# Five of six pairs of modulation vectors on VectorE as folded row sums, in tasks between the dense units

## The chip, the cores and the metric

The kernel runs on one core of a Trainium2 chip. The metric is the device time of one execution in microseconds (us). A core has TensorE (PE: matrix products, written to PSUM), VectorE (DVE), ScalarE (ACT), GpSimd (POOL) and SyncE (SP), which here only issues DMAs. Each engine runs its own instructions in order; they wait for each other by semaphores.

## The reference

A network of two layers and a closing block for 512 tokens of width 1024, with 256 context tokens beside them. The change touches only the modulation vectors:

```python
for l in range(DEPTH):                       # DEPTH = 2, D = 1024
    mod = silu_c @ w_ada[l] + b_ada[l]       # (1, 1024) @ (1024, 6144)
    sh1, sc1, gt1, sh2, sc2, gt2 = [m[:, None, :] for m in jnp.split(mod, 6, axis=-1)]
    modc = silu_cc @ w_ada[l] + b_ada[l]     # the same for the context
    shc1, scc1, gtc1, shc2, scc2, gtc2 = jnp.split(modc, 6)
    hc = modulate(rmsnorm(xc, g_mix[l]), shc1, scc1)
    h = modulate(rmsnorm(x, g_mix[l]), sh1, sc1)      # h * (1 + scale) + shift
    p = h @ w_in[l]
    x = x + gt1 * latent_mixer(p, ...)                # attention, convolution, gates, w_out
    h2 = modulate(rmsnorm(x, g_ffn[l]), sh2, sc2)
    x = x + gt2 * expert_choice_ffn(h2, ...)          # router, 16 experts
    # the context goes the same way in layer 0; in layer 1 it only gives keys and values
```

## The kernel before

**Stages.** For each layer: projection (one "values" unit, ten rotary units `("r", n)`, twelve convolution units `("c", fp, part, f)`), attention, merge (24 gate units `("g", br, d)`, numbered t = 8·br + d, after every second of them one branch unit `("b", br, d)` of two products; then eight output units `("o", d)`), choice (norm, router product, softmax, top-k, gathering of rows) and experts. The closing block follows. Layer 0 works on T = 768 columns (tokens and context), layer 1 after its keys on 512.

**A dense unit** is 128 output features: its weights (512 KB) come from HBM into the ring, ScalarE rounds them into a high part (`act_high`, L556), VectorE takes the difference as a low part (`dve_low`, L565), and TensorE multiplies high·high, high·low and low·high over eight slices of 128 rows (`pe_linear3`, L592: 48 matmuls of 512 or 256 columns at T = 768). The parts have two buffers: unit u+1 can be rounded once unit u−1 is multiplied, so VectorE's low part has one unit's length of room, less what ScalarE takes.

**The ring** has six slots of 512 KB (`halves`). SyncE issues the DMAs in the order of the list that `mixer_weights` builds, and piece p waits until piece p−6 has been read (`sp_dense`). A split piece is free when VectorE has taken its low part, a modulation piece when its product is done. Behind the list of layer 0 SyncE loads expert weights (`sp_experts`): three places of the old ring when they are free, four more once TensorE has done the second norm's sum, the rest after the gather.

**Modulation.** Both layers' vectors are made in layer 0. They are six pairs (pair = 3·layer + n2) of 2048 columns of `w_ada`, each 16 tiles of 128 x 1024: `pe_mod` (L665) multiplies a tile with the 32-column operand `csv` (column 0 the silu of c, column 1 that of c_ctx, the rest zero), four matmuls that run side by side on 32 columns of the array, and accumulates in one PSUM bank over eight tiles; `act_mod` (L675) copies the bank to SBUF, `pe_modt` (L683) turns it (four transposes), and `dve_mod` (L694, L700) adds the bias and makes the gain. Pair 0 is done in the start. Tiles 16 to 47 (pairs 1 and 2) follow two by two behind the ten rotary units and the first six convolution units, tiles 48 to 63 (pair 3) two by two in the first eight gate units, tiles 64 to 67 behind the last output unit, and 68 to 95 (the rest of pair 4 and pair 5) stand in `pe_choice`: 68 to 79 ahead of the router product (L1498), 80 to 87 ahead of its sum (L1507), 88 to 95 and pair 5's turn ahead of the product that turns the top-k indices (L1536 on).

**VectorE** has, by stage: in a convolution unit of part 2 the four operations L1029 to L1038, in one of part 0 the product L1043; in the gates the weighing L1429 (GpSimd adds the weighed product to the sum, L1471); in an output unit the update L1459 (GpSimd adds squares, L722). After the convolution it goes into the attention, whose first step is the row maximum L1094.

## Time and profile before

| what | value |
|---|---|
| median of 3 runs | 3527.2 us (3522.58 to 3527.33) |
| profiled execution: time / span | 3522.45 us / 3520.6 us |
| mean granted TensorE clock | 0.978 of full speed |
| busy: TensorE, weight loads, VectorE, ScalarE, GpSimd | 3278.1, 2200.8, 1242.5, 1004.9, 221.8 us |
| chain that ended last, by engine | TensorE 81%, DMA 10%, VectorE 4%, ScalarE 3%, issue 1% |
| HBM read | 606.54 MB |

The page cuts the span into 40 slices of 88 us; a digit is a share in tenths, 9 is 90% or more:

```profile
PE   6999999999799999989999996988879999989998
DVE  3335642233401011145563333111125444353333
PEclk9999999999799999999999998999999999989999
DMA  7540014221999999743102329999983121323331
```

Slices 1 to 4 hold the start and the projection of layer 0, 4 to 6 its attention, 6 to 10 its merge, 11 its choice, 11 to 18 its experts; layer 1's merge ends in slice 24, and its experts fill slices 25 to 30. The chain of waits is the part of the profile that says what the end of the span hung on: it starts at the last instruction and goes back, at each step to what released it. A view by time gives start, duration and, in brackets, how long the engine sat idle and for whom.

### The profile page before, as it was taken

The numbers are of one execution on the slowest core, as the hardware profiler recorded it, in microseconds if no ns is written. First come the engines' busy times: TensorE is split into PE (matmuls) and PEld (weight loads), VectorE is DVE, ScalarE is ACT, GpSimd is POOL, SyncE is SP. The second block draws the span as 40 slices with busy tenths as digits, with TensorE's granted clock in tenths as the row PEclk, the third lists the DMA queues.
The fourth block names the chain that finished last, engine by engine and source line by source line (L and its number), as shares of the span: only waits on it lengthen the run. The fifth ranks groups of instructions, "written<-read, shape, count | busy, mean of one in ns | idle before, by whom it ended". The sixth has DMA issues, their size and how long they took to land.

```text
span 3520.6 us, 48007 instructions
## 1 busy us (share of the span) xinstructions
PE 3278.1 (93%) x21250; PEld 2200.8 (63%) x21250; DVE 1242.5 (35%) x1821; ACT 1004.9 (29%) x1571; POOL 221.8 (6%) x142
## 2 busy tenths in 40 slices
PE   6999999999799999989999996988879999989998
PEld 5787667888334343467768882332328766858887
DVE  3335642233401011145563333111125444353333
ACT  3623541122210001037353222000022354342223
POOL 0100000121000000001000220000002010120000
PEclk9999999999799999999999998999999999989999
DMA  7540014221999999743102329999983121323331
GB/s 216 151 143 25 1 49 122 64 61 59 335 398 399 385 350 395 298 64 81 42 1 72 97 90 369 421 421 421 421 327 87 35 58 37 96 60 97 101 96 66
DMA packets 385614, 617.00 MB, mean 175 GB/s; under 512 B 99234, under 2 KB 288896, under 8 KB 360704
## 3 DMA queue, kind: packets, MB, share of 16 engines
q1 hardware_dynamic: 378064, 596.50, 47.9%
q0 software_dynamic: 4384, 15.73, 1.3%
q8 instruction: 168, 2.75, 0.3%
q10 hardware_dynamic: 2960, 1.71, 0.2%
q14 instruction: 38, 0.31, 0.0%
HBM read 606.54 MB, written 7.34 MB: 174 GB/s over the span
## 4 chain that ended last, share of the span: by engine, by line
PE 81%; DMA 10%; DVE 4%; ACT 3%; issue 1%; POOL 0%; ACTq 0%; SPq 0%; DVEq 0%
PE ps L592 32%; PE ps L1844 6%; PE ps L2228 5%; PE ps L1083 4%; DMA ring<-in_w_e_up 4%; PE ps L1172 3%; PE ps L1880 3%; PE ps L1847 3%; DMA ring<-in_w_e_down 3%; PE ps L1133 3%; PE ps L644 3%; PE ps L1347 3%; PE ps L1839 2%; PE ps L613 2%; PE ps L1885 2%; PE ps L1876 2%
## 5 line engine op out<-in xcount | busy, mean ns | idle before, releaser
L592 PE MATMUL ps<-xh,wh 128*128 128x512 f32 x1912 | 638.2, 372 | 19.4 <-DVE xl L2074 9.3
L592 PE MATMUL ps<-xl,wh 128*128 128x512 f32 x1912 | 630.7, 368 | 0.0
L592 PE MATMUL ps<-xh,wl 128*128 128x512 f32 x1912 | 630.2, 368 | 0.0
L565 DVE TENSOR_TENSOR wl<-ring,wh 128x1024 fp32r<-128x1024 f32 (+1 forms) x259 | 333.1, 1287 | 443.0 <-ACT wh L556 441.4
L592 PEld LDWEIGHTS ps<-xh,wh 128*128 128x128 f32 x1912 | 330.6, 189 | 101.3 <-issue 23.8
L556 ACT ACTIVATE wh<-ring 128x1024 fp32r<-128x1024 f32 (+1 forms) x259 | 271.9, 1050 | 421.1 <-PE ps L592 161.7
L592 PEld LDWEIGHTS ps<-xh,wl 128*128 128x128 f32 x1912 | 330.6, 189 | 61.0
L592 PEld LDWEIGHTS ps<-xl,wh 128*128 128x128 f32 x1912 | 330.2, 189 | 58.7 <-issue 0.5
L1844 PE MATMUL ps<-ring,arena 128*32 128x512 f32 x1344 | 177.6, 600 | 0.9 <-ACT arena L1592 0.9
L1839 PE MATMUL ps<-ring,arena 128*64 128x512 f32 x704 | 163.2, 605 | 12.4 <-DMA ring<-in_w_e_up 8.0
L1094 DVE TENSOR_REDUCE sm<-ps 128x2 f32<-128x1536 f32 (+3 forms) x96 | 142.3, 1482 | 42.0 <-PE ps L1083 41.6
L1083 PE MATMUL ps<-arena 64*128 64x256 f32 (+3 forms) x800 | 150.9, 451 | 2.6 <-DVE arena L1043 1.8
L1112 ACT ACTIVATE tmp<-ps,sm 128x768 f32<-128x768 f32 (+3 forms) x176 | 132.7, 763 | 46.5 <-DVE sm L1097 39.0
L1133 PE MATMUL ps<-consts,tmp 128*128 128x128 f32 x832 | 126.8, 284 | 20.5 <-DVE arena L1189 12.2
L2005 DVE SCALAR_TENSOR_TENSOR y<-ps,aff,y 128x1024 fp32r<-128x1024 f32 x16 | 20.5, 1284 | 306.9 <-ACT y L1936 306.9
L1471 POOL TENSOR_TENSOR arena<-arena,tmp 128x768 f32<-128x768 f32 (+1 forms) x32 | 65.8, 2059 | 980.5 <-DVE tmp L1429 980.5
L1133 PEld LDWEIGHTS ps<-consts,tmp 128*128 128x128 f32 x832 | 88.3, 141 | 59.0 <-issue 21.8
L1839 PEld LDWEIGHTS ps<-ring,arena 128*64 128x64 f32 x704 | 48.4, 138 | 115.5 <-issue 80.4
L1876 PE MATMUL ps<-ring,arena 128*64 128x512 f32 x360 | 93.7, 596 | 21.7 <-DMA ring<-in_w_e_down 13.7
L1172 PE MATMUL ps<-arena 128*64 128x256 f32 (+1 forms) x896 | 99.6, 368 | 14.6 <-DVE arena L1156 14.6
L1156 DVE COPY arena<-ps 128x512 f32<-128x512 f32 (+1 forms) x136 | 87.2, 657 | 69.9 <-PE ps L1133 69.9
L1083 PEld LDWEIGHTS ps<-arena 64*128 64x128 f32 (+1 forms) x800 | 86.8, 187 | 38.0 <-issue 28.4
(277 smaller groups left out, 4437.1 us busy)
## 6 DMA issues: line engine op xcount, KB each, us to landing
ring<-in_w_e_gate SPq DMA_DIRECT2D x87, 1024.0 KB, 19.7
ring<-in_w_e_up SPq DMA_DIRECT2D x85, 1024.0 KB, 20.2
ring<-in_w_e_down SPq DMA_DIRECT2D x85, 1024.0 KB, 20.7
ring<-in_w_in SPq DMA_DIRECT2D x112, 512.0 KB, 3.9
ring<-in_w_ada SPq DMA_DIRECT2D x96, 512.0 KB, 4.9
arena<-in_w_e_up SPq DMA_DIRECT2D x43, 1024.0 KB, 17.7
arena<-in_w_e_down SPq DMA_DIRECT2D x43, 1024.0 KB, 20.1
arena<-in_w_e_gate SPq DMA_DIRECT2D x41, 1024.0 KB, 20.4
```

Of the source, the lines that this page charges most:

```text
L556: e.activation(in_heads(X, u, m.WH[:, o:o + many]), heads_of(X, u, halves.aps[s], many), ACT.Copy).then_inc(*hi.up(X.key, q))
L565: e.tensor_tensor(in_heads(X, u, m.WL[:, o:o + many]), heads_of(X, u, halves.aps[s], many), in_heads(X, u, m.WH[:, o:o + many].bitcast(F32 ...
L592: i = e.matmul(ps[0:M, a:b], w[:, k, 0:M], h[:, k, a:b], start=k == 0 and p == 0, stop=k == 7 and p == 2)
L1083: x = e.matmul(ps[:, col:col + k.shape[-1]], q, k, start=first, stop=last, skip_group_check=True)
L1094: e.tensor_reduce(mx, A.units(i, A.scores(i)), AX, ALU.max).then_inc(*a_rm.up(A.stage, i))
L1112: e.activation(dst[:, u], src[:, u], ACT.Exp, bias=A.small(i, 1)[:, u:u + 1], scale=s["scale"], accum_out=A.small(i, 2)[:, u:u + 1]).then_ ...
L1133: x = e.transpose(ps[:, 128 * c:128 * c + 128], src[:, u, 128 * b:128 * b + 128], ident)
L1172: e.matmul(ps[r0:r0 + 64, q0:q1], v, pt, start=x == 0, stop=x == len(pv) - 1, skip_group_check=True)
L1839: i = e.matmul(pa[64 * h:64 * h + 64, 512 * w:512 * w + 512], rows_of(1, kk, x, 0, 64), W[:, k, 512 * h:512 * h + 512], start=kk == 0, sto ...
L1844: e.matmul(pa[64 * h + g:64 * h + g + 32, 512 * w:512 * w + 512], rows_of(0, kk, x, g, g + 32), W[:, k, 512 * h:512 * h + 512], start=kk = ...
L1876: i = e.matmul(ps[64 * x:64 * x + 64, 512 * h:512 * h + 512], HT2[p % 2][:, x, k % 4, k // 4, :], w, start=k == 0, stop=k == 7)
L2228: i = e.matmul(ps[:, n:n + 512], ff_part(h, f)[c], w[:, 0, n:n + 512], start=f == 0 and p == 0, stop=f == 31 and p == 2, skip_group_check= ...
```

## The change

Pair 0 stays as it is. The other five pairs leave TensorE: each is cut into four groups of 512 columns (20 groups, `MODS`), and a group into five tasks. Tasks 0 to 3 each take a piece of 256 rows x 512 columns (512 KB, as before; 80 pieces as before) and add the rows, scaled by `csv`, into an accumulator of 128 x 512: for each of two slices of 128 rows and each vector one VectorE operation, `scalar_tensor_tensor` (the first slice `tensor_scalar`). Pairs 1 to 3 have two vectors, pairs 4 and 5 one (layer 1's context needs none of theirs). Task 4 (the turn) does for each vector a transpose of 128 x 512 in blocks of 32 x 32 and a row sum over 32 columns (128 x 16 remains). When a pair's four groups are done, `pe_fold` adds the four blocks of partitions by four matmuls of 32 (or 16) columns with the widened constant `fold`, and `dve_fold` adds the bias and makes the gain.

The tasks stand at the end of the VectorE work of single units: layer 0's convolution units (2, 1 or 2 tasks for part 1, 2, 0; pair 1), layer 0's gate units (2 in even t, 1 in odd t, none in t = 7 and 15) and output units 0 to 2 (2 each) for pairs 2 and 3; layer 1's convolution units 0 to 9 (1 each) and gate units (30 tasks from t = 0 to 20) for pairs 4 and 5. The pieces stand in the ring's list behind the weights of the unit after; no modulation piece is left in the rotary units, behind the output units or in the choice stage. Folds: in layer 0 at t = 0, t = 16 and output unit 5, in layer 1 at t = 8 and 22. ScalarE's five copies go.

```diff
+        MR0 = TR = tmp[:, 3840:4352]
+        ACC = [tmp[:, 4352 + 512 * i:4864 + 512 * i] for i in (0, 1)]
+        RS = tmp[:, 5376:5632].rearrange("p (s q w b) -> p s q w b", s=2, q=4, w=2)
+        MODS = [(pair, q) for pair in range(1, 6) for q in range(4)]
+        vectors = lambda g: (0, 1) if MODS[g][0] < 4 else (0,)
...
+        def mod_quarter(g, c):
+            pair, q = MODS[g]
+            o = 2048 * (pair % 3) + 512 * q
+            return piece(I["w_ada"][pair // 3][256 * c:256 * c + 256, o:o + 512])
+
+        def spread(groups, slots):
+            tasks = iter([(g, c) for g in groups for c in range(5)])
+            return {slot: [x for _, x in zip(range(many), tasks)] for slot, many in slots}
+
+        beside_conv = lambda many: [(("c", j), many[j // 2 % 3]) for j in range(12)]
+        beside_gates = [(("t", t), 0 if t in (7, 15) else 2 - t % 2) for t in range(24)]
+        TASKS = [{**spread(range(4), beside_conv((2, 1, 2))),
+                  **spread(range(4, 12), beside_gates + [(("o", d), 2) for d in range(3)])},
+                 {**spread(range(12, 14), [(("c", j), int(j < 10)) for j in range(12)]), **spread(range(14, 20), beside_gates)}]
+        FOLDS = [{("t", 0): 1, ("t", 16): 2, ("o", 5): 3}, {("t", 8): 4, ("t", 22): 5}]
...
+            for m in range(16) if l == 0 else ():
+                X.raw(("mod", m), *mod_source(m), p_mod, "mod", m)
+
+            def mods(parts):
+                for g, c in parts:
+                    if c == 4:
+                        continue
+                    X.raw(("mods", g, c), *mod_quarter(g, c), d_md, "mod", g, 2 * c + 1, vectors(g)[-1])
...
-                if j < 16:
-                    mods(16 + 2 * j, 17 + 2 * j)
+                if j > 9:
+                    mods(TASKS[l]["c", j - 10])
...
-                    if t < 8:
-                        mods(48 + 2 * t)
...
+                    mods(TASKS[l]["t", t])
             for d in range(KD):
                 X.split(("o", d), 128, column(I["w_out"][l], 128 * d))
-            mods(*range(64, 96))
+                mods(TASKS[l].get(("o", d - 1), []))
...
+        def dve_mod_part(e, X, g, c):
+            if c == 4:
+                return dve_mod_turn(e, g)
+            s, srcs, many, kind, what, arrived = X.pieces[X.plain["mods", g, c]]
+            e.wait_ge(*arrived)
+            for k in (2 * c, 2 * c + 1):
+                src = halves.aps[s][:, 512 * (k % 2):512 * (k % 2) + 512]
+                for w in vectors(g):
+                    if k == 0:
+                        if g:
+                            e.wait_ge(*d_md.at("turn", g - 1, w if w in vectors(g - 1) else 0))
+                        e.tensor_scalar(ACC[w], src, csv[:, 0, w:w + 1], None, ALU.mult).then_inc(*d_md.up("mod", g, k, w))
+                        continue
+                    e.wait_ge(*d_md.at("mod", g, k - 1, w))
+                    e.scalar_tensor_tensor(out=ACC[w], in0=src, scalar=csv[:, k, w:w + 1], in1=ACC[w], op0=ALU.mult,
+                                           op1=ALU.add).then_inc(*d_md.up("mod", g, k, w))
+
+        def dve_mod_turn(e, g):
+            pair, q = MODS[g]
+            if q == 0 and pair > 2:
+                e.wait_ge(*p_modt.at("mod", pair - 2))
+            for w in vectors(g):
+                e.wait_ge(*d_md.at("mod", g, KD - 1, w))
+                if w or g:
+                    e.wait_ge(*(d_md.at("sum", g, 0) if w else d_md.at("sum", g - 1, vectors(g - 1)[-1])))
+                e.transpose(TR, ACC[w]).then_inc(*d_md.up("turn", g, w))
+                e.wait_ge(*d_md.at("turn", g, w))
+                e.tensor_reduce(RS[:, pair % 2, q, w], TR.rearrange("p (b i) -> p b i", i=32), AX, ALU.add).then_inc(*d_md.up("sum", g, w))
+
+        def pe_fold(e, pair):
             ps, when = bank.take(("modt", pair), d_mod.at("mod", pair, 1))
             for w in when:
                 e.wait_ge(*w)
-            e.wait_ge(*c_mod.at("mod", pair))
-            for c in range(4):
-                i = e.transpose(ps[:, 128 * c:128 * c + 128], MR(pair)[:, 128 * c:128 * c + 128], ident)
+            g = MODS.index((pair, 3))
+            many = len(vectors(g))
+            e.wait_ge(*d_md.at("sum", g, many - 1))
+            sums = RS[:, pair % 2, :, 0:many].rearrange("p q w (k g) -> p g q w k", g=4)
+            for g in range(4):
+                i = e.matmul(ps[32 * g:32 * g + 32, 0:16 * many].rearrange("p (q w k) -> p q w k", q=4, w=many), K("fold"), sums[:, g],
+                             start=True, stop=True)
             i.then_inc(*p_modt.up("mod", pair))
 
-        def dve_mod(e, pair):
+        def dve_fold(e, pair):
             l, n2 = pair // 3, pair % 3
+            many = len(vectors(MODS.index((pair, 3))))
             e.wait_ge(*p_modt.at("mod", pair))
-            pv = bank.of["modt", pair][:, 0:512].rearrange("p (n h g w) -> p n g h w", n=2, h=2, g=4)
-            for nb in (0, 1):
-                j0 = 16 * n2 + 8 * nb
-                o = modv[:, l, j0:j0 + 8, :].rearrange("p (g h) w -> p g h w", h=2)
-                b = PT[:, 32 + 48 * l + j0:40 + 48 * l + j0].rearrange("p (g h) -> p g h", h=2)
-                e.tensor_tensor(o, pv[:, nb, :, :, 0:2], b.unsqueeze(3).broadcast_to([128, 4, 2, 2]),
-                                ALU.add).then_inc(*d_mod.up("mod", pair, nb))
+            ps = bank.of["modt", pair][:, 0:16 * many].rearrange("p (q w k) -> p q k w", q=4, w=many)
+            o = modv[:, l, 16 * n2:16 * n2 + 16, 0:many].rearrange("p (q k) w -> p q k w", q=4)
+            b = PT[:, 32 + 48 * l + 16 * n2:48 + 48 * l + 16 * n2].rearrange("p (q k) -> p q k", q=4)
+            e.tensor_tensor(o, ps, b.unsqueeze(3).broadcast_to([128, 4, 4, many]), ALU.add).then_inc(*d_mod.up("mod", pair, 1))
             if n2 != 1:
-                m = n2 // 2
-                g = PT[:, 16 * m + 8 * l:16 * m + 8 * l + 8].unsqueeze(2).broadcast_to([128, 8, 2])
-                e.wait_ge(*d_mod.at("mod", pair, 1))
-                e.scalar_tensor_tensor(out=A1v[:, l, m], in0=modv[:, l, 24 * m + 8:24 * m + 16, :], scalar=1.0, in1=g,
-                                       op0=ALU.add, op1=ALU.mult).then_inc(*d_mod.up("mod", pair, "A"))
+                dve_gain(e, pair, many)
...
-                    if l == 0 and t == 8:
-                        pe_modt(e, 3)
                     pe_linear3(e, X, ("g", br, d), 128, T, (X.key, "g", t), g_sg.at(X.key, t))
-                    if l == 0 and t < 8:
-                        pe_mod(e, 48 + 2 * t)
+                    if ("t", t) in FOLDS[l]:
+                        pe_fold(e, FOLDS[l]["t", t])
...
+                if ("o", d) in FOLDS[l]:
+                    pe_fold(e, FOLDS[l]["o", d])
...
+                for task in TASKS[l]["c", j]:
+                    dve_mod_part(e, X, *task)
...
+                    if ("t", t - 1) in FOLDS[l]:
+                        dve_fold(e, FOLDS[l]["t", t - 1])
...
+                    for task in TASKS[l]["t", t]:
+                        dve_mod_part(e, X, *task)
...
+                for task in TASKS[l].get(("o", d), []):
+                    dve_mod_part(e, X, *task)
+                if ("o", d - 1) in FOLDS[l]:
+                    dve_fold(e, FOLDS[l]["o", d - 1])
...
-            mods(*range(68, 80))
...
-            mods(*range(80, 88))
...
-            mods(*range(88, 96))
-            if l == 0:
-                pe_modt(e, 5)
...
-                act_mod(e, 4)
```

## Rows read from the trace of the kernel before

**Rows 1.** Groups of instructions: shapes xcount | busy us, mean ns | idle, releaser.
```profile
L665 PE MATMUL ps<-ring,cs 128*32 128x256 f32 x768 | 57.7, 409 | 13.3 <-DMA ring<-in_w_ada 13.1
```

**Rows 2.** TensorE by time, one rotary unit: start us, us, what.
```profile
106.78 1.07 PE L665 MATMUL ps<-ring,cs 128*32 128x256 f32 x16
107.78 1.56 PE L889 MATMUL ps<-tmp,consts 128*128 128x512 f32 x4
```

**Rows 3.** Chain of waits, convolution units of layer 0: start us, us, what.
```profile
205.76 8.68 PE ps L592 x48
215.43 8.68 PE ps L592 x48
...
253.58 42.42 PE ps L592 x240
```

**Rows 4.** Chain of waits, gate units of layer 0.
```profile
521.25 8.67 PE ps L592 x48
...
549.40 8.68 PE ps L592 x48
...
596.47 8.66 PE ps L1347 x48
608.72 18.34 PE ps L592 x96
627.06 8.46 PE ps L1347 x48
...
652.48 8.48 PE ps L1347 x48
```

**Rows 5.** Chain of waits, router stage of layer 0, in its own window.
```profile
898.74 2.63 PE ps L1498 x32
...
902.27 6.78 DMA ring<-in_w_ada
...
909.73 1.46 PE ps L1507 x12
...
923.37 7.85 DMA ring<-in_w_ada
```

**Rows 6.** Chain of waits, whole span, its 195 longest pieces: neighbours around the experts.
```profile
936.67 8.19 DMA taken<-h2d,aff
1492.29 3.47 PE ps L1880 x16
```

**Rows 7.** Chain of waits, router stage of layer 1: its ends.
```profile
2104.78 9.09 PE ps L592 x40
...
2159.90 9.57 PE ps L1839 x32
```

**Rows 8.** VectorE by time, router stage of layer 0: the normalised rows.
```profile
887.76 8.56 DVE L1629 SCALAR_TENSOR_TENSOR arena<-arena,A,tmp 128x512 f32<-128x512 f32 x16 [6.59 <-ACT tmp L753]
```

**Rows 9.** VectorE groups by form: shapes xcount | busy us, mean ns.
```profile
L918 DVE STREAM_SHUFFLE tmp<-tmp 128x512 f32<-128x512 f32 x32 | 23.5, 734 | 0.0
...
L2079 DVE SCALAR_TENSOR_TENSOR tmp<-arena,PT,tmp 128x512 f32<-128x512 f32 x16 | 18.1, 1141 | 6.0 <-ACT tmp L753 5.6
...
L1034 DVE SCALAR_TENSOR_TENSOR tmp<-tmp,PT 128x511 f32<-128x511 f32 x8 | 6.0, 751 | 0.3
```

**Rows 10.** VectorE by time, one convolution product unit.
```profile
214.47 0.95 DVE L1029 TENSOR_TENSOR tmp<-tmp,ps 128x768 f32<-128x768 f32 x1 [6.66 <-PE ps L592]
...
218.23 1.22 DVE L565 TENSOR_TENSOR wl<-ring,wh 128x1024 fp32r<-128x1024 f32 x1
```

**Rows 11.** VectorE by time, a low part in the second gate branch.
```profile
636.71 2.87 DVE L565 TENSOR_TENSOR wl<-ring,wh 128x1024 fp32r<-128x1024 f32 x1
```

**Rows 12.** GpSimd by time, the same moment.
```profile
636.66 1.84 POOL L1471 TENSOR_TENSOR arena<-arena,tmp 128x768 f32<-128x768 f32 x1 [1.49 <-DVE tmp L1429]
```

**Rows 13.** All engines by time, entry of the first attention.
```profile
296.03 0.95 DVE L1043 TENSOR_TENSOR arena<-tmp,ps 128x768 f32<-128x768 f32 x1 [6.10 <-PE ps L592]
...
298.74 1.76 DVE L1094 TENSOR_REDUCE sm<-ps 128x2 f32<-128x1536 f32 x1 [1.76 <-PE ps L1083]
```

107 lines of the change are left out of this document (40 added, 67 removed).

## The prediction

> **What bounds the kernel now.** I read the chain of waits first, then TensorE by time where the modulation stands, then VectorE in the units that get the tasks. The chain is TensorE for 81% of the span, and in layer 0's dense units it is TensorE without a gap. So a microsecond of products taken from those units is a microsecond of time, as long as nothing else ends last there. In the choice stage the chain is another: twice it stands on the arrival of a piece of `w_ada` for about 7 us [rows 5], while TensorE's own work is short. In layer 0's experts TensorE bounds again: after the gather the next long piece of the chain that isn't one of many short TensorE pieces comes at 1492 us, and no DMA stands between [rows 6]. So what is won ahead of the experts should stay won, though the stage reads weights at nearly the rate of the queues (385 to 399 GB/s on the page).
>
> A group view is of little use for the size: it gives the modulation products 57.7 us of busy time [rows 1], but they overlap their neighbours, and a third of them lies in the choice stage.
>
> **What is removed.**
>
> *Rotary units.* Two tiles begin at 106.78 and the next product begins at 107.78: 1.00 us for two tiles [rows 2]. Ten units: 10.0. Pair 1's turn in one of them goes too, 0.4 by its four transposes (half of what two tiles take, as an estimate). Cover: the next unit's weights are rounded in time here: nothing of VectorE's or ScalarE's releases L592 in these units, so the gain is taken whole. **10.4 us.**
>
> *Convolution units.* With two tiles the units follow each other at 9.67 us; five units without tiles take 42.42, which is 8.48 each [rows 3]. The difference is 1.19, six times, and a turn of 0.4: **7.6 us.**
>
> *Gate units, first branch.* Two gate units and a branch unit with four tiles take 28.15 us (521.25 to 549.40); without tiles 25.42 (627.06 to 652.48) [rows 4]. 2.73, four times: **10.9 us.**
>
> *Between the branches.* The branch unit at 596.47 ends at 605.13, its last tile at about 605.7, and the next gate unit only begins at 608.72 [rows 4]. ScalarE's high part for that unit is queued behind its copy of pair 3's products, which waits for the last tile; both go. That is 3.0 us, and 1.4 more, since the two units that follow take 18.34 us instead of 2 x 8.48 [rows 3, 4]: TensorE had stood still and began again at the lower of its two clocks. **4.4 us.**
>
> *Choice stage.* 64 to 67 go from behind the output units: about 1.0 on the chain. The rows of the router product are ready when VectorE has passed them on (887.76 + 8.56 = 896.3) [rows 8] and ScalarE about 0.8 later (768 columns, an estimate by VectorE's rate for them); the product then needs some 0.7 at the lower clock, the copy 1.0 and the sum up to 2.0, so the sum would end near 900.7 less the 1.0 above, 899.7. It ended at 909.73 + 1.46 = 911.19 [rows 5]. That is 11.5 in all. The last tiles waited until 923.37 + 7.85 = 931.2 [rows 5], and pair 5's copy and turn behind them put off the product that turns the indices by 1.9, counted from the end of the top-k. Then the gather: 8.19 us from issue to landing [rows 6], while seven expert pieces of 1 MB, issued at the same moment, share the queues. With the list 16 MB shorter these are in before the gather starts. The gather alone: bounds 0 and 4.5 us less (nearest are single 512 KB pieces of weights at 3.9 us in the page's issues); I take 3. **16.4 us.** As a cross-check, layer 1's choice stage without tiles takes 2159.90 - 2113.87 = 46.0 [rows 7]. With its sizes for 768 instead of 512 columns I get 51 for layer 0, which now takes 67.4. That is 16 too.
>
> Sum of the gains: 10.4 + 7.6 + 10.9 + 4.4 + 16.4 = **49.7 us.**
>
> **What is added.**
>
> *The price of a task.* A multiply-add of 128 x 511 takes 0.751 us [rows 9]. Two vectors alternate, so one needn't wait for the one before it. Of 512 and 256 columns, sixteen unchained ones take 8.56 us [rows 8]; by columns that is 0.66 for 512 with the overlap. A product task with two vectors is 4 x 0.66 = 2.65; with one vector the two are chained, 2 x 0.79 = 1.6. A block transpose isn't in the trace. Bounds: half and twice the shuffle across the same 32 rows, which has 0.734 [rows 9]; as the nearest row I take that, and the same for the row sum. A turn is then 2 x 1.5 = 3.0, with one vector 1.5. In all 12 x (4 x 2.65 + 3.0) + 8 x (4 x 1.6 + 1.5) = some 226 us of VectorE.
>
> *Room in the convolution units.* In a unit of part 2 VectorE works from 214.47 to 218.23 behind the unit's end and then takes the low part, 1.2 [rows 10]. Laid out unit by unit with 8.48 for each: 3.9 + 3.0 (a turn) + 1.2 = 8.1 of 8.48; part 0: 1.1 + 5.3 + 1.2 = 7.6, with a turn 8.0; part 1 is free sooner. So each task just fits, and nothing or 1 us is lost; I take **0.5**. With turns of 4.5 the same layout loses 3.5.
>
> *Entry of the attention.* The last convolution unit has two tasks (2.65 + 3.0), and they stand on VectorE ahead of the first row maximum, which began at 298.74, 1.8 after the unit's product ended [rows 13]. It would begin at 297.0 + 5.65 = 302.7: 4.0 later, and everything in the attention waits for it. With 0.5 for TensorE's clock after the longer pause: **4.5.** This is the dearest of the added parts.
>
> *Gates of layer 0.* The tightest place is the branch unit's low part: from the end of the last unit VectorE has its weighing 1.1, one task 2.65, a low part 1.2, two tasks 5.3 and a low part 1.2 = 11.5 of the 17.0 that two gate units take. GpSimd adds the weighed product in the second and third branch, and the row shows what that does: a low part took 2.87 us instead of 1.22 [rows 10, 11] where an addition of 1.84 ran from the same moment [rows 12]. That is 1.65 more: 13.1 of 17.0. Nothing is lost. The Trainium skill, "SBUF — State Buffer", section "Who interferes with whom", says why: a VectorE instruction with two SBUF inputs contends with a GpSimd instruction that reads SBUF, and one blocks while the other runs. The rule speaks against this change, since every multiply-add here has two SBUF inputs; by it as by the rows the loss per unit is at most one addition of GpSimd.
>
> *Output units.* Here it decides: 1.3 for the update, 5.3 to 5.65 for two tasks, 1.2 for the low part and up to 1.7 for GpSimd's sum of squares is 9.5 to 9.9 of 8.35 in units 1 and 2. By the order of the units the second overrun only adds what the first didn't already give: **2.2**, with the last gate unit's task ahead of the last low parts.
>
> *Layer 1.* Gates: room as above. Convolution: a unit has 5.5 us (two thirds of 8.3); own work 2.7 by columns, a turn 1.5 and the low part 1.2 fill it, with a few tenths over: **0.5.**
>
> *Folds.* Four small matmuls each, about 0.5, five times: **2.5.** The DMA amount is unchanged (80 pieces of 512 KB); layer 1 gets 16 MB where the page shows under 100 GB/s, and its expert prefetch hangs on TensorE's norm sum, not on the list.
>
> Sum of the costs 0.5 + 4.5 + 2.2 + 0.5 + 2.5 = **10.2.** Net 39.5, so 3522.45 - 39.5 = **3483 us** for an execution like the profiled one, which lies 5 below the median of the runs and at their lowest.
>
> **Rivals.**
>
> *A, deeper: 3473.* The gather lands in half the time, the folds vanish in the stream, and the units keep the faster pace that the rotary units show (8.32 against 8.48, cause unknown). For: nothing competes for the queues any more. Against: the pace isn't tied to anything that the change touches.
>
> *B, VectorE late in places: 3494.* A transpose at its upper bound or dearer multiply-adds lengthen turns to 4.5: 3.5 in the convolution, 1.5 at the attention, 3 in the output units, 3 in layer 1. For: the room is 0.4 us in the convolution. Against: shuffle and multiply-add rows.
>
> *C, the choice stage's gain is given back in the experts: 3499.* They begin 16 us earlier, and the queues, not TensorE, then set their pace. For: the rate on the page. Against: seven pieces are in sooner, and no DMA is on the chain today [rows 6].
>
> *D, slower: 3542.* VectorE ends last in every unit that has tasks. A multiply-add of the same size takes 1.141 us in another access pattern [rows 9]. At that price a task is 4.6, and a gate cycle runs into its branch unit: 1.1 + 4.6 + 1.65 + 1.2 + 9.1 + 1.2 = 18.9 of 17.0, 1.9 lost twelve times, 23; by the same layout 10 in the convolution, 9 in the output units and attention, 17 in layer 1. These 59 come on top of the forecast, 3483 + 59, so 20 slower than before. Units run over from about 1.0 per multiply-add on, and the gain is gone near 1.1. Against: these tiles are contiguous, as those of the 0.751 row.
>
> *E, no change: 3522.* What went from TensorE was hidden anyway. Against: the paces with and without tiles [rows 3, 4].
>
> The Trainium skill, "VectorE: DVE Perf Modes", section "Rules for kernel authors", advises to restructure a `tensor_reduce` on a hot path as the slowest operation; no row of a 512-column row sum from SBUF is in this trace, and B is what would follow.
>
> **How the numbers follow.** Forecast 0.62, A 0.13, B 0.14, C 0.05, D 0.04, E 0.02. The likeliest time is 3483; its own range is 3476 to 3490. The range for 8 in 10 reaches over A and into B: 3469 to 3497. A measurement of this kernel can tell about 0.2% from no change. Faster by more than that: 0.94; within it 0.02; slower 0.04.
>
> **What would show it.** Right: no wait of TensorE on `w_ada`; convolution and rotary units at the pace without tiles; the first row maximum some 6.7 us after the last convolution unit; router stage near 51 us; VectorE busy near 1465 us. A wrong step shows as idle time of TensorE ahead of L592 released by VectorE's low part (B, D) or by a DMA in the experts (C), and as the duration of the multiply-add, the transpose and the row sum. I would be wrong above all if these run slower than their nearest rows, or if the tasks' pieces, freed by VectorE, hold up weights behind them in the ring.

## The result, and the profile after the change

| what | before | after |
|---|---|---|
| median | 3526.93 us (3522.58 to 3527.33) | 3484.86 us (3480.73 to 3485.78) |
| ratio | | 0.9879, interval 0.9867 to 0.9892 |
| span of the profiled execution | 3520.6 us | 3483.8 us |
| VectorE busy | 1242.5 us | 1442.8 us |
| TensorE busy | 3278.1 us | 3233.3 us |
| mean granted TensorE clock | 0.978 | 0.980 |

The kernel became 1.2% faster: 3483 was forecast, 3484.86 measured. The spans of the two profiled executions differ by 36.8 us where the steps of the prediction give 39.5.

First the page of the kernel after: busy time of the engines, the chain by engine, and the groups of the new VectorE work (shapes and count | busy us, mean ns of one | idle time before).

```profile
PE 3233.3 (93%) x20626; PEld 2182.4 (63%) x20630; DVE 1442.8 (41%) x2136; ACT 1002.0 (29%) x1566; POOL 226.2 (6%) x142
...
PE 80%; DMA 9%; DVE 6%; ACT 3%; issue 1%; POOL 0%; ACTq 0%; SPq 0%; DVEq 0%
```

```profile
L735 DVE SCALAR_TENSOR_TENSOR tmp<-ring,cs,tmp 128x512 f32<-128x512 f32 x224 | 167.4, 796 | 1.9
...
L746 DVE STREAM_TRANSPOSE tmp<-tmp 128x512 f32<-128x512 f32 x32 | 22.6, 707 | 0.5
L748 DVE TENSOR_REDUCE tmp<-tmp 128x16 f32<-128x512 f32 x32 | 21.9, 686 | 1.1
```

VectorE got 228 us of new instructions (these rows and 15.9 of the first slices' L732; 226 was the sum of the prediction) and is busy 41% of the span, and still ends last in only 6% of the chain. Its busy time is 1442.8 us where the prediction looked for 1465; 14.5 of the missing 22 are the low parts, which took 333.1 us before and 318.6 after. The block transpose and the row sum, for which the trace before had no row, take 0.707 and 0.686 us; the shuffle at 0.734 in [rows 9] was a good neighbour for both.

Then the chain of waits of the kernel after (start us, us, what), at the places of [rows 3] (convolution), [rows 4] (gates), [rows 5] (choice) and [rows 6] (gather).

```profile
176.55 101.77 PE ps L612 x576
...
480.79 8.59 PE ps L612 x48
...
506.63 16.95 PE ps L612 x96
523.58 8.32 PE ps L1398 x48
...
582.43 16.95 PE ps L612 x96
...
838.96 17.18 PE ps L612 x96
...
874.75 1.50 PE ps L1551 x12
...
899.90 4.14 DMA taken<-h2d,aff
```

The twelve convolution units stand there as one piece of 101.77 us, which is 8.48 each: no task of VectorE made TensorE wait in them. The output units end at 838.96 + 17.18 = 856.14. A gate cycle (two gate units and a branch unit) takes 25.27 instead of 28.15. Between the branches nothing stands still: 582.43 follows the branch unit of 574.11 + 8.32. No arrival of `w_ada` is on the chain, and the gather lands after 4.14 us instead of 8.19.

By stage, each from the start of its first dense unit in the chain to that of the next stage (the output units are counted from the end of the last branch unit to their own end):

| stage | before | after | gain | forecast |
|---|---|---|---|---|
| start, to the first rotary unit | 77.88 | 79.74 | -1.9 | none |
| rotary units | 108.88 | 96.81 | +12.1 | +10.4 |
| convolution units | 109.24 | 101.77 | +7.5 | +7.6 - 0.5 |
| attention, to the first gate | 197.02 | 202.47 | -5.5 | -4.5 |
| gates, first branch, and boundary | 115.70 | 101.64 | +14.1 | +10.9 + 4.4 - 0.5 |
| gates, second and third branch | 203.0 | 202.6 | +0.4 | -0.5 |
| output units | 68.3 | 71.1 | -2.8 | -2.2 - 0.5 |
| choice, to the first expert product | 67.4 | 50.4 | +17.0 | +16.4 |
| experts of layer 0 and norm | 601.2 | 600.9 | +0.3 | 0 |
| layer 1, values to first gate | 318.9 | 321.2 | -2.3 | -0.5 |
| the rest of layer 1 | | | -2.1 | -1.0 |

(A fold is 0.5, as the prediction has it, five times.) The last line is the 36.8 of the spans less the 38.9 by which the first gate of layer 1 begins earlier.

### The profile page after: what moved, and what is told of

Same layout as the page of the kernel before. It is cut to its first block, busy times and chain, and to the rows that moved or that the text cites. A ratio compares the mean times of both kernels' runs of the same rounds, so it can differ in the third digit from the quotient of the medians.

```text
span 3483.8 us, 47130 instructions
## 1 busy us (share of the span) xinstructions
PE 3233.3 (93%) x20626; PEld 2182.4 (63%) x20630; DVE 1442.8 (41%) x2136; ACT 1002.0 (29%) x1566; POOL 226.2 (6%) x142
## 4 chain that ended last, share of the span: by engine, by line
PE 80%; DMA 9%; DVE 6%; ACT 3%; issue 1%; POOL 0%; ACTq 0%; SPq 0%; DVEq 0%
PE ps L612 32%; PE ps L1876 6%; PE ps L2260 5%; PE ps L1134 4%; DMA ring<-in_w_e_up 4%; PE ps L1223 3%; PE ps L1912 3%; PE ps L1879 3%; PE ps L664 3%; DMA ring<-in_w_e_down 3%; PE ps L1184 3%; PE ps L1398 3%; PE ps L1871 2%; PE ps L633 2%; PE ps L1917 2%; PE ps L1908 2%
## 5 line engine op out<-in xcount | busy, mean ns | idle before, releaser
L585 DVE TENSOR_TENSOR wl<-ring,wh 128x1024 fp32r<-128x1024 f32 (+1 forms) x259 | 318.6, 1230 | 296.6 <-ACT wh L576 295.9
L1871 PE MATMUL ps<-ring,arena 128*64 128x512 f32 x704 | 163.1, 605 | 12.7 <-DMA ring<-in_w_e_up 8.1
L735 DVE SCALAR_TENSOR_TENSOR tmp<-ring,cs,tmp 128x512 f32<-128x512 f32 x224 | 167.4, 796 | 1.9
L1223 PE MATMUL ps<-arena 128*64 128x256 f32 (+1 forms) x896 | 99.6, 368 | 14.6 <-DVE arena L1207 14.6
```

Source lines behind the costliest of these rows:

```text
L585: e.tensor_tensor(in_heads(X, u, m.WL[:, o:o + many]), heads_of(X, u, halves.aps[s], many), in_heads(X, u, m.WH[:, o:o + many].bitcast(F32 ...
L735: e.scalar_tensor_tensor(out=ACC[w], in0=src, scalar=csv[:, k, w:w + 1], in1=ACC[w], op0=ALU.mult, op1=ALU.add).then_inc(*d_md.up("mod", g ...
L1223: e.matmul(ps[r0:r0 + 64, q0:q1], v, pt, start=x == 0, stop=x == len(pv) - 1, skip_group_check=True)
L1871: i = e.matmul(pa[64 * h:64 * h + 64, 512 * w:512 * w + 512], rows_of(1, kk, x, 0, 64), W[:, k, 512 * h:512 * h + 512], start=kk == 0, sto ...
```

## The experiments

Each kernel ran beside the kernel before on the same chip. The median of the kernel before was 3524.93 us (3523.24 to 3525.91) beside the first four kernels, 3527.9 (3523.26 to 3530.19) beside the next four and 3525.71 (3519.71 to 3528.32) beside the last two. So medians of different groups can be compared to some 3 us only; a smaller difference from the changed kernel rests on the stages of the chains.

**What do the five pairs still cost?** The first kernel leaves pairs 1 to 5 out, products and loads, so layer 1 and the second half of layer 0 compute with shift and gate 0 and gain 1.

```diff
             def mods(parts):
-                for g, c in parts:
+                for g, c in ():
...
         def dve_mod_part(e, X, g, c):
+            return
...
```

> The changed kernel with pairs 1 to 5 left out altogether (no load, no task, no fold; their shifts and gates are zero and their gains one), so it shows what is won by taking the products away, without the price of what replaced them. Theory: the stretches of the changed kernel without its own losses, 5.5 at the attention, 2.8 in the output units, 1.6 in layer 1's convolution and 1.5 to 2.5 for the folds: about 3472 (51 below before; the prediction's sum of gains was 49.7). Rival (products largely hidden, and the added work costs nothing): about 3484.

Measured: 3472.39 us (3471.54 to 3473.22), ratio 0.9851 (0.9835 to 0.9867), span 3471.4. As expected (3472): without the pairs the kernel before would be 52.5 us shorter, and the form on VectorE costs 12.5 of that by the medians (3484.86 - 3472.39) and 12.4 by the spans (3483.8 - 3471.4); by the two ratios it is some 10. The chain of this kernel says where:

```profile
176.55 101.77 PE ps L612 x576
...
476.71 17.23 PE ps L612 x96
...
781.85 66.81 PE ps L612 x384
...
892.44 4.05 DMA taken<-h2d,aff
...
1592.42 65.33 PE ps L612 x288
```

The convolution is as long as in the changed kernel, so 20 tasks cost nothing there. The first gate comes 4.1 us sooner, and that is the attention alone. From there to the end of the output units it is 371.95 against 375.35: 3.4. The gather is the same. Layer 1 is 2.5 shorter up to its first gate, and its twelve convolution units are one piece of 65.33; the rest is 2.1 shorter.

**Is the attention's loss the queue on VectorE?** The second kernel moves the last four tasks of pair 1 from convolution units 10 and 11 to the first gate units; the later tasks move up, so that gate units 1, 3, 5 and 7 have one more. The group that lies half on either side of the attention is overwritten there, so that part of pair 1 isn't computed as in the reference.

```diff
-        TASKS = [{**spread(range(4), beside_conv((2, 1, 2))),
-                  **spread(range(4, 12), beside_gates + [(("o", d), 2) for d in range(3)])},
+        many_conv = [2, 2, 1, 1, 2, 2, 2, 2, 1, 1, 0, 0]
+        many_gate = [2, 2, 2, 2, 2, 2, 2, 1, 2, 1, 2, 1, 2, 1, 2, 0, 2, 1, 2, 1, 2, 1, 2, 1]
...
-        FOLDS = [{("t", 0): 1, ("t", 16): 2, ("o", 5): 3}, {("t", 8): 4, ("t", 22): 5}]
+        FOLDS = [{("t", 4): 1, ("t", 16): 2, ("o", 5): 3}, {("t", 8): 4, ("t", 22): 5}]
```

> The changed kernel, but the last four tasks of pair 1 (three products' worth and the turn) stand in gate units 0 and 1 instead of convolution units 10 and 11; the later tasks of the gates move up, with one more task in t = 1, 3, 5 and 7, and pair 1's fold stands at t = 4. Theory (the entry of the attention): VectorE's 5.4 us of tasks ahead of the first row maximum are what the attention lost, so the stretch from the end of the last convolution unit to the first gate unit falls from 202.5 back to about 197.5 us, and the time from 3484.9 to about 3480. Rival (the attention lost its 5.5 us to something else, the clock or the ring): the stretch stays within 1 us of 202.5 and the time within 1 us.

Measured: 3480.93 us (3479.76 to 3484.74), ratio 0.9878 (0.9861 to 0.9894), span 3479.7. The medians lie 3.9 apart, the spans 4.1; the ratios (0.9878 and 0.9879) don't tell the two kernels apart. The evidence is the stretch from the last convolution unit to the first gate, which went from 202.5 to 198.4, where 197.5 was expected. What it lost in the changed kernel shows in VectorE and TensorE by time (start us, us, engine, line; in brackets idle time and what ended it):

```profile
278.34 0.95 DVE L1093 TENSOR_TENSOR arena<-tmp,ps 128x768 f32<-128x768 f32 x1 [1.09 <-PE ps L612]
279.21 2.73 DVE L735 SCALAR_TENSOR_TENSOR tmp<-ring,cs,tmp 128x512 f32<-128x512 f32 x4
...
281.86 0.70 DVE L746 STREAM_TRANSPOSE tmp<-tmp 128x512 f32<-128x512 f32 x1
...
284.67 1.75 DVE L1145 TENSOR_REDUCE sm<-ps 128x2 f32<-128x1536 f32 x1
...
287.78 0.69 PE L1184 MATMUL ps<-consts,tmp 128*128 128x128 f32 x2 [5.58 <-ACT tmp L1163]
```

The product of the unit is taken over at 278.34, and then one task and a turn run, 5.5 us, ahead of the first row maximum. This begins 6.4 us after the unit's end; before it was 2.7 [rows 13]. TensorE stands still for 5.6 us and waits for ScalarE, which waits for that maximum.

That is 3.6 us, and the stretch lost 5.5. The rest goes with TensorE's granted clock, which can be read in the eleven profiles without doubled multiply-adds. These rows take the 18 us from the end of the last convolution unit on; the number behind the brackets is the granted clock. They are of the kernel before, the kernel with no pairs, the changed kernel, and two that come below: the fifth (no task ahead of the attention) and the kernel before with cut products.

```profile
296.00:314.00 18.00, 13.94 (x99) 1.00 0.00 1
278.32:296.32 18.00, 14.30 (x90) 0.91 0.01 1
278.32:296.32 18.00, 11.20 (x52) 0.81 0.28 83
279.21:297.21 18.00, 13.93 (x99) 1.00 0.00 1
297.28:315.28 18.00, 14.59 (x80) 0.81 0.01 1
```

| tasks ahead of the attention | granted clock in the 18 us | attention, to the first gate |
|---|---|---|
| none: before, fourth and fifth kernel | 1.00 | 197.0, 196.8, 196.8 |
| none: no pairs, tasks moved, last design | 0.91 | 198.4, 198.4, 198.1 |
| none: before with cut products | 0.81 | 199.5 |
| two: changed kernel (twice), third kernel, held pieces | 0.81 | 202.5, 202.3, 202.2, 202.3 |

Without tasks at the entry the clock falls to its lower level in some executions and not in others, even of the same code (first and third line), and that costs 1.0 to 2.5 us. With the two tasks it fell in all four profiles. So the changed kernel's 5.5 are 3.6 of queue and some 1.8 of clock.

**Are the output units' tasks free in fuller gates?** The third kernel takes all tasks out of the output units and the last gate unit, and puts a second task into the odd gate units of branches 0 and 1.

```diff
...
+        many_gate = [2, 2, 2, 2, 2, 2, 2, 1, 2, 2, 2, 2, 2, 2, 2, 0, 2, 1, 2, 1, 2, 1, 2, 0]
+        many_out = [0, 0, 0]
...
+        FOLDS = [{("t", 0): 1, ("t", 16): 2, ("o", 1): 3}, {("t", 8): 4, ("t", 22): 5}]
```

> The changed kernel, but without tasks in gate unit 23 and in the output units; these seven stand in odd gate units (two tasks each in t = 1, 3, 5, 9, 11 and 13, one in 7), and pair 3's fold at output unit 1. Theory (the output units overrun because tasks and GpSimd's additions stand ahead of the low parts): end of the last branch unit to end of the last output unit falls from 71.1 to about 68.3 us, the time by about 3 to 3482. The fuller gate units don't lose anything (13.1 + 2.65 of 17.0 by the prediction's layout). Rival (VectorE has no room in the gates either): what is won there is lost in the gate units, and the time stays or rises.

Measured: 3484.91 us (3482.02 to 3485.57), ratio 0.9886 (0.9869 to 0.9902), span 3482.4, no shorter than the changed kernel by the medians. The expectation was wrong in two places. The output units fell from 71.1 to 70.1, where 68.3 was expected, and from the first gate to the end of the last branch unit the kernel lost 2.7 (306.96 instead of 304.3), in the second branch. Its chain there:

```profile
608.43 3.72 DVE tmp L739 x4
...
612.67 2.73 DVE tmp L739 x4
615.40 1.15 DVE wl L589
...
616.68 8.72 PE ps L616 x48
```

The unit after the branch unit waits for its low part (L589), which is queued behind two tasks. After the branch unit's end at 607.46 VectorE has 1.0 of weighing, then 7.0 for two tasks (5.5 alone; the first is drawn out to 3.72 by GpSimd's addition, and 0.5 passes before the second), then 1.2 for the low part: it ends 9.1 later, and a gate unit lasts only 8.5. So the first two cycles there take 26.3 and 26.1 instead of 25.3. In branch 0, where GpSimd adds nothing, the same two tasks cost nothing.

The fourth kernel joins the two edits and fills the third branch too (again with one group of pair 1 across the attention, where it is not computed as in the reference).

> Both moves: layer 0's convolution units 10 and 11, gate unit 23 and the output units have no task; every gate unit from 0 to 22 has two, but 7 and 15 have one. Theory: the two gains add, 5 + 3, and the time is about 3477. With two tasks in every gate unit VectorE's layout has 15.8 of 17.0 us, so it just fits. Rival: the gates run over, a microsecond or more per pair of units, and the time is 3485 to 3495.

Measured: 3486.44 us (3483.36 to 3490.95), ratio 0.9893 (0.9877 to 0.991). Missed by 9 us, from the same cause: the stall of one us now stands in the third branch as well (in its chain 3.72 us pieces of L739 at 735.42 and 761.68). The attention gives 5.7 us (196.8), and from the first gate to the end of the output units 5.9 are lost again (381.3 instead of 375.35). The fifth added to this layer 1: no task in convolution units 0, 2, 3, 8, 9 and 11, four more beside the gates.

> As the variant with both moves in layer 0, and in layer 1 the convolution units 0, 2, 3, 8, 9 and 11 have no task (six stand in units 1, 4, 5, 6, 7 and 10, the others in the gates, two each in t = 1, 3 and 5). Theory: layer 1's convolution, 66.9 us in the changed kernel, goes back to 65.4, and the time is 1.5 below that variant, about 3475.5. Rival: layer 1's gate units have no room for second tasks, and it is no better than that variant.

Measured: 3486.37 us (3485.41 to 3486.78), ratio 0.9884 (0.9867 to 0.99). Also missed by the time (3475.5 was expected, and it is no faster than the fourth kernel), but its part of layer 1 came true: the twelve units of the convolution are one piece of 65.33 us, where the changed kernel has 66.9. What it cost there the chain of the changed kernel shows:

```profile
1609.49 0.75 DVE tmp L735
1610.24 1.15 DVE wl L585
1611.52 11.16 PE ps L612 x48
1622.79 32.96 PE ps L612 x144
```

The third unit waits for a low part that stands behind two operations of the first unit's task, and two later units wait by 0.1. Each stop costs somewhat more than its idle time (the 48 matmuls behind it take 11.16 and 11.18 instead of 10.9), so that together they make 1.6.

**How near is the edge?** Each multiply-add twice (the first result is thrown away).

```diff
...
+                    e.scalar_tensor_tensor(out=TR, in0=src, scalar=csv[:, k, w:w + 1], in1=src, op0=ALU.mult,
+                                           op1=ALU.add).then_inc(*d_md.up("extra", g, k, w))
                     e.wait_ge(*d_md.at("mod", g, k - 1, w))
                     e.scalar_tensor_tensor(out=ACC[w], in0=src, scalar=csv[:, k, w:w + 1], in1=ACC[w], op0=ALU.mult,
...
```

> The changed kernel with every multiply-add of the tasks issued twice (the second one writes a tile that nothing reads). It tests the room in the units. Theory (a unit pays once VectorE's own work, the tasks and the next low part exceed its length): a task with two vectors is 5.3 instead of 2.65 us, which by the prediction's layout overruns in the convolution by 11, at the attention by 2.7 more, in the gates of branches 1 and 2 by 1.6 to 3 per pair of units (13 to 20), in the output units by 13 and in layer 1 by about 9: 3535, between 3520 and 3545, so at or above the kernel before. Rival (VectorE at 41% of the span has room for 148 us more, wherever it stands): about 3488.

Measured: 3542.25 us (3536.22 to 3542.65), ratio 1.0038 (1.0024 to 1.0053), span 3540.5. So at twice the price of a multiply-add the change would have lost, by a little; 3535 was expected, between 3520 and 3545. The rival by which TensorE would still hide most of it (3488) is refuted. Rows of its chain:

```profile
504.25 8.74 PE ps L612 x48
...
888.78 17.17 PE ps L612 x96
```

The units no longer run into one piece: the convolution and the attention lose 23.5 (the first gate starts at 504.25 instead of 480.79), the gates and output units 26.4 (the last ends at 888.78 + 17.17 = 905.95 instead of 856.14). VectorE is busy for only 143 us more (1586.1), and 57 of them come out at the end.

**Why is the gather faster?** The next kernel holds the first seven expert pieces until the indices are turned, so that they are issued at the gather's time as in the kernel before.

```diff
                 elif s < KEPT:
...
+                    if l == 0:
+                        e.wait_ge(*p_n.at("f0", KD - 1))
+                        e.wait_ge(*p_rt.at("e0", "ix"))
```

> The changed kernel, but layer 0's first seven expert pieces are issued only when the indices are turned, at the moment of the gather, as they were before the change. Theory (the gather landed in 4.1 instead of 8.2 us because it has the queues to itself): its landing goes back to about 8.2 us, and the time rises by 4, to 3489. Rival (the gather is shorter for another reason, such as the pieces of the modulation that are gone): landing stays near 4.1 and the time near 3485.

Measured: 3492.45 us (3488.58 to 3493.43), ratio 0.9901 (0.9885 to 0.9918), 7.6 more than the changed kernel by the medians. Its chain:

```profile
900.75 9.15 DMA taken<-h2d,aff
...
967.50 20.03 DMA ring<-in_w_e_down
...
1033.80 19.90 DMA arena<-in_w_e_down
```

The gather takes 9.15 us again, so its 4 us of gain is the emptier queue and nothing of the gather itself. Two arrivals of expert weights come onto the chain, which is how rival C would have looked; the changed kernel has neither, with its pieces in ahead of the gather. In this profile they cost nothing in sum: from the gather's landing to layer 1's values it takes 602.3 us (909.90 to 1512.20), in the changed kernel 603.4 (904.04 to 1507.46). The profiled execution (3488.58) is also the fastest of the four; the other three lie at 3491.8 to 3493.4 and have no trace. So 5.0 of the 7.6 are shown, the gather; where the rest goes is not.

**Was it the products or their arrival in the choice stage?** The kernel before, with tiles 64 to 95 loaded and waited for, but each product cut to one matmul of 8 columns (so pairs 4 and 5 aren't computed).

```diff
+            if m >= 64:
+                i = e.matmul(ps[0:32, 256 * nb:256 * nb + 8], csv[:, k, :], w[:, 0:8], start=k == 0, stop=k == 7)
-            for g in range(4):
+            for g in range(4 if m < 64 else 0):
```

> The kernel before, but of the 32 modulation tiles 64 to 95 only the loads and the waits for their arrival are kept; their products are one matmul of 8 columns each, so pairs 4 and 5 are not computed. Theory (the choice stage hung on the arrival of the pieces, not on TensorE's work): the stage from the last output unit to the first expert product stays within 3 us of its 67.4, and the time is 3523 to 3527. Rival (it hung on the products): the stage falls by about 15 us, and the time is about 3512.

Measured: 3520.53 us (3518.99 to 3524.17), ratio 0.9983 (0.9973 to 0.9992), span 3517.2. Chain of the choice stage:

```profile
904.03 6.09 DMA ring<-in_w_ada
910.43 2.69 PE ps L1509 x12
...
936.72 8.03 DMA taken<-h2d,aff
```

The output units end at 882.33 here, so the sum (L1509) ends 30.8 us later, against 31.2 before and 20.1 after the change: nearly all of those 11 us were the arrival of the pieces, not TensorE's work on them. The gather takes 8.03 as before. From the sum to the gather it is 23.6 instead of 25.5, as in the changed kernel (23.65): the 1.9 of the prediction. Pair 5's copy and turn are still in this kernel, but they end at the same moment as the top-k (934.07 and 934.02), since the last pieces come 1.3 us sooner behind the sum and their products are 0.8 shorter; so it doesn't tell how much of the 1.9 was arrival. The stage took 65.0 us instead of 67.4, within the 3 us expected; the time is 7 below the 3527.9 beside it (3.4 by the spans of the two profiles) and 2.5 under the range expected, and only 2.4 of that is the stage.

**Can both places be mended?** The last design puts whole groups on either side of the attention, and second tasks only into odd units of branch 0, where GpSimd adds nothing.

```diff
+        TASKS = [{**spread(range(3), [(("c", j), (2, 2, 1, 1, 2, 2, 2, 2, 1, 0, 0, 0)[j]) for j in range(12)]),
+                  **spread(range(3, 12), [(("t", t), {1: 2, 3: 2, 5: 2, 7: 1}.get(t, many)) for (_, t), many in beside_gates]
+                           + [(("o", d), (2, 2, 2, 1)[d]) for d in range(4)])},
+                 {**spread(range(12, 13), [(("c", j), int(j in (1, 4, 5, 6, 7))) for j in range(12)]),
+                  **spread(range(13, 20), [(("t", t), 2 if t == 1 else many) for (_, t), many in beside_gates])}]
+        FOLDS = [{("t", 4): 1, ("t", 16): 2, ("o", 5): 3}, {("t", 12): 4, ("o", 1): 5}]
```

> Whole groups only on either side of the attention, nothing left out: layer 0's convolution units carry 15 tasks (units 0 to 8: 2, 2, 1, 1, 2, 2, 2, 2, 1) instead of 20, the gates 38 (a second task in units 1, 3 and 5 and one in unit 7 of branch 0, where no GpSimd addition runs yet), the output units 7 (2, 2, 2, 1); pair 1 is folded behind gate unit 4. In layer 1 five tasks instead of ten lie beside the convolution (units 1, 4, 5, 6, 7), 35 beside the gates, and pair 5 is folded behind output unit 1. My theory (the attention's first rows queue behind the last tasks; layer 1's 1.6 us are the product behind the shared operand's low part at units 0 to 2; second tasks are free only where VectorE has no neighbour on GpSimd): attention stretch 198 instead of 202.5, layer 1's convolution 65.3 instead of 66.9, no stall in the gates, 3484.9 - 4.1 - 1.6 = 3479, between 3476 and 3482. Rival 1 (a second task in an odd gate unit costs about 1 us wherever it stands): 3 to 4 us lost in branch 0, 3482 to 3484. Rival 2 (the attention's gain was due to pair 1's last group being handled differently in that other kernel): 3483 to 3485, the stretch still 202.

Measured: 3477.3 us (3476.42 to 3480.77), ratio 0.9863 (0.9846 to 0.9879), span 3478.8. The chain:

```profile
476.35 17.21 PE ps L614 x96
...
582.00 3.47 DVE qol L1384 x4
...
1595.20 65.33 PE ps L614 x288
```

It hit the expectation (3479, between 3476 and 3482). The attention stretch is 198.05, layer 1's convolution 65.33. Branch 0 has two tasks in odd units and keeps its cycle of 25.27 us (501.88 to 527.15), which refutes rival 1; the stretch refutes rival 2. Between the first two branches 0.4 us go, where the turn now stands ahead of the next branch's low parts (L1384). Layer 1's first gate comes 7.5 sooner than in the changed kernel; of that 0.9 goes up to the last expert weights' arrival and 1.6 in the closing attention (2668.93 + 34.56 to 2753.80 is 50.3, in the changed kernel 48.7), which has the same code: the granted clock was 0.97 there, with 0.57 for some 4 us, and 1.00 in the changed kernel. The span is 5.0 shorter, the median 7.6 lower. The intervals of the two ratios overlap (0.9846 to 0.9879 and 0.9867 to 0.9892), so that it beats the changed kernel rests on the stages as much as on the times, and on the one execution of the changed kernel beside it, which took 3484.15.

The changed kernel itself ran once more beside it, to see what moves between executions of one program.

> The changed kernel unaltered, for a second profile of one and the same program: it tells what moves from execution to execution. If the 1.9 us that the start lost (first rotary product at 79.74 instead of 77.88) is scatter of the first transfers, it starts anywhere between 78 and 81; if it belongs to the program, at 79.7 within 0.2. If the two paces of the 768-column units (8.32 and 8.48 us) belong to the program, each stretch shows the same one as in the first profile (gates of branches 1 and 2 at 16.95 for two units, branch units at 8.32); if they are a state of the execution, at least one stretch changes to the other.

Measured: 3484.15 us, span 3482.2. The first rotary product starts at 79.40. Over the nine profiles whose starts have the code of the changed kernel it lies between 78.77 and 80.32, and in the kernel before with cut products at 79.15, where the kernel before itself has 77.88. So most of the 1.9 us of the start is scatter: the first weights' arrival and the value products vary by a us or so. With two profiles of the old start, a part of up to 1 us that belongs to the program isn't excluded. The gates' paces came out the same as in the first profile, 16.95 and 8.32; the first three rotary units went over to the other pace (16.97 and 8.48 instead of 16.65 and 8.32), so it doesn't belong to the program alone.

## Why the prediction was right, point by point

**The mechanism** was right: in dense units TensorE's time is the kernel's time, and what was taken from it came out whole. The paces of units with and without tiles gave convolution (7.5 measured, 7.6 less 0.5 predicted; 1.19 six times and 0.4 are 7.5, not 7.6) and gates with the boundary (14.1 against 14.8). Of the boundary's 4.4 the 1.4 of TensorE's clock are not a thing of the code: the kernel before with cut products has the same wait there and goes on at a granted clock of 1.00, with 16.88 us for the two units (612.50), where the kernel before had 0.52 in the first 3.3 us and 18.34.

**Rotary units, 12.1 instead of 10.4.** The term took the distance of two starts, 1.00 us for two tiles [rows 2]. The pace of the units went from 10.81 to 9.61, so 1.20 each: the neighbours lost 0.2, which stands in no row of the tiles. By the starts, half of it lies between the last dense product and what follows it (0.45 with tiles, 0.34 without) and half behind the next products, L889 (1.20 and 1.10 to the dense unit). For the other units the prediction had compared paces with and without tiles and got it right. That is the same quantity read in two ways, and only the second includes the neighbour.

**Choice stage, 17.0 instead of 16.4.** Its steps hold singly. The sum ended 11.1 sooner relative to the output units' end (11.5 forecast), the turn of the indices gave 1.85 (1.9), the gather 4.05 where 3 was taken between 0 and 4.5. The cut products show that the first was arrival, the held pieces that the last was the shared queues. The 3 of the gather was chosen within its bounds, and the 4.05 lies near their upper end.

**Attention, 5.5 instead of 4.5.** The queue is the one named: the two tasks took 5.5 (5.65 forecast), and the row maximum began 3.6 later after the unit's end than before (4.0 forecast). The term that was too small is the 0.5 for TensorE's clock after the longer pause. The granted clock was 0.81 over the first 18 us, against 1.00 before, and that cost some 1.8. It isn't all due to the tasks: with no task at the entry the clock fell as well in four profiles of seven, and the stretch then took 198.1 to 199.5 instead of 197.0. Against those with 0.91 the tasks cost 4.1 to 4.4, which agrees with the forecast only because the part of the clock that is compared is smaller.

**Gates.** That a cycle has room for three tasks held. The sum over both gate units (13.1 of 17.0) was the wrong test for more than that: the low part of the second unit has its own due time one unit, 8.5 us, after the branch unit. The change happens to keep to it with one task in odd units; the third kernel with two doesn't.

**Output units, 2.8 with the fold.** The place and the sum were right (2.2 and 0.5), the parts less so. Some 0.9 of the 2.8 is no wait: the last five units, which have no tasks, take 42.6 (813.52 to 856.14), where the kernel with no pairs runs all eight in 66.81, 41.8 for five. 0.24 of this is the fold, and the rest a slower pace. The kernel with no tasks in the output units is slow there too (17.18 + 51.09 = 68.3 for the eight), so the pace isn't a queue; that kernel won back 1.0 of the 2.8 and no more.

What the wait consists of shows by time. VectorE has four products in a gate unit of the second branch (4.32 us together), and four at the first output unit beside GpSimd's two additions (5.05 together); alone they take 2.73. Single records of them, and of GpSimd at the output unit:

```profile
608.67 0.75 DVE L735 SCALAR_TENSOR_TENSOR tmp<-ring,cs,tmp 128x512 f32<-128x512 f32 x1
609.34 2.33 DVE L735 SCALAR_TENSOR_TENSOR tmp<-ring,cs,tmp 128x512 f32<-128x512 f32 x1
611.59 0.74 DVE L735 SCALAR_TENSOR_TENSOR tmp<-ring,cs,tmp 128x512 f32<-128x512 f32 x1
...
787.33 1.47 DVE L735 SCALAR_TENSOR_TENSOR tmp<-ring,cs,tmp 128x512 f32<-128x512 f32 x1
788.72 2.33 DVE L735 SCALAR_TENSOR_TENSOR tmp<-ring,cs,tmp 128x512 f32<-128x512 f32 x1
```

```profile
785.50 2.76 POOL L1521 TENSOR_TENSOR arena<-arena,tmp 128x768 f32<-128x768 f32 x1 [22.60 <-DVE tmp L1473]
788.21 2.30 POOL L1521 TENSOR_TENSOR arena<-arena,tmp 128x768 f32<-128x768 f32 x1
```

It is single instructions that get longer, and only where they meet one of the other engine. In the gate unit the first product (0.75) ran ahead of the addition, the second began while the addition ran and ended 0.55 behind its end, and the next has its 0.74 again. At the output unit two products are long, one for each addition. An addition that begins beside a running low part or product takes 2.3 to 2.8 us, one that comes first 1.84 [rows 12]. The Trainium skill, "SBUF — State Buffer", section "Who interferes with whom", has one of them blocked while the other runs, and the order of issue decides which. The trace agrees: the 2.33 of the second product are the 1.78 that the addition still ran, and 0.55 of its own. In the gates of the second branch the toll on four products is 1.6 (4.32 instead of 2.73), as the prediction had it from [rows 11].

**Layer 1, 2.3 instead of 0.5, and 2.1 after it.** The convolution's 1.6 is mostly a low part that comes late for the third unit, behind the first unit's task. The prediction had seen a few tenths of overrun per unit, and missed that at the start of the stage nothing has been laid up. Another 0.8 lies between the convolution and layer 1's first gate (161.6 us, 160.8 before), where no task stands: the clock fell in both kernels, in the changed one for longer (up to the first of the products L1223 it is 15.3 us, 14.5 before). Behind the first gate the 2.1 split so: 0.8 until the first arrival of expert weights that is on the chain (2268.74 us before, 2230.70 after; the merge lies in it, and its two folds are the 0.8), 0.9 over the experts, and 0.4 in the rest. From that arrival on the chain hangs on the queues in both kernels, eleven waits of 24 to 29 us, so that stretch takes what its transfers take, whatever starts it. Rival C's mechanism thus acts in layer 1, but it starts by when its inputs come and passes the gain on nearly whole. In layer 0, for which C was proposed, the experts took 590.4 instead of 590.8.

**Folds, 2.5.** They cost less, some 1.8 for the five. In the chain two gate units with a fold between them take 11.32 us in layer 1 instead of 10.91 (1895.56 to 1906.88) and 17.37 in layer 0 instead of 16.95 (683.50 to 700.87), so 0.4 each. The first gate cycle is 0.3 longer than in the kernel with no pairs, and the fold in the output units is a piece of 0.24.

**The rivals.** A (3473) is what the kernel with no pairs costs, 3472.39, so it would have needed all tasks to be free. Its first two conditions came nearly true (the gather in 4.1 us, folds at 1.8), the tasks' waits did not vanish. B's price was wrong (a turn took 2.9, not 4.5). D's mechanism is real, as the doubled multiply-adds show, but that they took 3542.25 where D gave 3542 is chance: D reckoned with 1.141 us for a multiply-add, and two of 0.744 (the median) are 1.49, so its layout had lost too much for its price. C did not happen in layer 0. E is refuted by the convolution and gate rows above.

**Sum.** By the stages the shorter ones give 51.4 (49.7 forecast, folds and overruns in the same stages not yet taken off), the longer ones take 12.7 (10.2 forecast), and the start takes 1.9 more. The forecast stood on the time of the profiled execution, 3522.45, near the lowest of its kernel; the profiled execution after was the highest of its own (3485.78). The net was 2.7 too large by the spans, and the base 4.5 below the median of the kernel before; that the median hit to 2 us is in part luck, these two errors cancelling. Two things in the sum were luck in themselves: the profiled execution before had the low clock between the branches and not at the attention, and the changed one the other way round.

## What to carry to other kernels

Read what a foreign piece of work costs on TensorE from the pace of the units with and without it, not from its own rows: it includes what the neighbours lose. When work moves to an engine that is half idle, its total fits long before its due times do: lay out what is queued ahead of each operand that TensorE needs next, unit by unit, and look for the places where a stage begins with that engine's result (here the attention's first row maximum), since there even one task is on the path. And a task costs more beside a busy GpSimd than its own rows say. Before a us or two is put down to a change of code, compare the granted clock of the stretch in both profiles: here it moved by itself by as much.

## What the runs showed of the hardware that was not expected

- The block transpose of fp32, 128 x 512 in blocks of 32 x 32, takes 0.707 us, as long as a multiply-add (0.746 the median), and a row sum over 32 columns of the same tile 0.686.
- Where VectorE's multiply-adds meet GpSimd's additions, the one that comes second is drawn out by the rest of the first: a multiply-add to 2.33 from 0.74 us, an addition to 2.3 to 2.8 from 1.84; their neighbours keep their time.
- TensorE's clock at the entry of an attention differs between executions of the same code: 1.00 and 0.81 over the same 18 us in two profiles, and the stretch took 197.0 and 199.5 us.
- A gather of rows lands in 4.0 to 4.4 us in an empty queue and in 8.0 to 9.2 with 7 MB of weights issued at the same moment.
- Full units of 768 columns run at two paces, 8.32 and 8.48 us (16.95 for two), both at a granted clock of 1.00 in the stretches. The profile of the same program repeated them in the gates, where the branch units have 8.32 after the change and had 8.46 before it in the second branch [rows 4]. In the rotary units they moved: the first two took 16.65 in one execution and 16.97 in the other. What sets them is open.
